# Three signals for a unit's transposed components, and a quad's compression in one run, in the sample-score stage of a hybrid decoder step

## The reference

```python
def compress_blocks(kseq, pe, w1, w2):          # CMP_STRIDE 16, HD 64
    ...
    ch = kp.reshape(B, nc, CMP_STRIDE, KH, HD).transpose(0, 1, 3, 2, 4).reshape(B, nc, KH, CMP_STRIDE * HD)
    ha = ch @ w1[:half]
    hb = ch @ w1[half:]
    h = ha[:, :-1] + hb[:, 1:] + pe.reshape(-1) @ w1
    return jax.nn.silu(h) @ w2
```

## Time and profile before

| | us |
|---|---|
| timed runs, median of 3 | 3030.18 (3027.63 to 3040.13) |
| profiled execution | 3035.08 |
| its span | 3033.3 |
| TensorE busy | 2729.7 (90%) |
| its weight loads busy | 2222.7 (73%) |
| DVE / ACT / POOL busy | 917.5 / 577.9 / 238.8 |
| turns, L979, both layers | 216.2 in 1600 records |
| compression, L1009, both layers | 288.8 in 4352 records |

### The profile page before, as it was taken

One profiled execution on the slowest core, in us unless ns is written; L12 is line 12 of the kernel. 1 busy time (PEld: TensorE's weight loads), 2 busy tenths in 40 slices (PEclk: granted clock), 3 DMA queues, 4 the chain that ended last, 5 costly groups with the idle time before them and its releaser, 6 DMA issues. The chain is left out here.

```text
span 3033.3 us, 44988 instructions
## 1 busy us (share of the span) xinstructions
PE 2729.7 (90%) x17236; PEld 2222.7 (73%) x17236; DVE 917.5 (30%) x2207; ACT 577.9 (19%) x1224; POOL 238.8 (8%) x328
## 2 busy tenths in 40 slices
PE   6996999698698999999969879987977989999997
PEld 4875888466585888888758678865757768888885
DVE  2731333443543210000118223343544332010002
ACT  0012332223310200000110223322242103000002
POOL 0500000000030100000005000000002101000000
PEclk8997999799695999999979979997987879999998
DMA  6205775242001134022042256733410021341220
GB/s 194 75 28 151 212 216 176 73 123 81 2 22 50 44 109 125 28 69 71 0 138 70 49 177 215 217 112 105 125 48 1 22 91 35 108 122 28 56 56 30
DMA packets 343596, 276.93 MB, mean 91 GB/s; under 512 B 61473, under 2 KB 339106, under 8 KB 343002
## 3 DMA queue, kind: packets, MB, share of 16 engines
q1 hardware_dynamic: 316840, 253.71, 28.4%
q10 hardware_dynamic: 26546, 20.35, 2.2%
HBM read 264.14 MB, written 18.17 MB: 93 GB/s over the span
## 5 line engine op out<-in xcount | busy, mean ns | idle before, releaser
L2166 PE MATMUL psum<-xT,up_ring 128*128 128x272 f32 x2048 | 470.3, 392 | 0.0
L2166 PEld LDWEIGHTS psum<-xT,up_ring 128*128 128x128 f32 x2048 | 389.0, 190 | 80.3
L2185 PE MATMUL psum<-ff,HT 128*128 128x272 f32 x1536 | 353.6, 392 | 0.0
L2185 PEld LDWEIGHTS psum<-ff,HT 128*128 128x128 f32 x1536 | 291.8, 190 | 60.2
L368 PE MATMUL psum<-xT,w_ring 128*128 128x272 f32 x1408 | 327.4, 396 | 7.4 <-PEq L161 4.0
L368 PEld LDWEIGHTS psum<-xT,w_ring 128*128 128x128 f32 x1408 | 269.7, 192 | 65.0 <-issue 4.7
L979 PE MATMUL psum<-cst,cache 128*128 128x128 f32 x1600 | 216.2, 286 | 14.0 <-DMA cache<-in_cache_nsa_kv 10.8
L979 PEld LDWEIGHTS psum<-cst,cache 128*128 128x128 f32 x1600 | 181.1, 146 | 32.9 <-DMA cache<-in_cache_nsa_kv 11.2
L2029 DVE SCALAR_TENSOR_TENSOR xT<-xT,psum 128x544 f32<-128x544 f32 (+1 forms) x42 | 24.2, 584 | 529.5 <-PE psum L2185 441.6
L1009 PEld LDWEIGHTS psum<-chunks,W 64*128 64x128 f32 x2304 | 144.0, 199 | 24.0 <-issue 24.0
L1009 PE MATMUL psum<-chunks,W 64*128 64x128 f32 (+1 forms) x2304 | 157.3, 289 | 0.0
(11 more groups left out here) (423 smaller groups left out, 3161.0 us busy)
## 6 DMA issues: line engine op xcount, KB each, us to landing
cache<-in_cache_nsa_kv SPq DMA_DIRECT2D x512, 192.0 KB, 2.7
up_ring<-in_w_up SPq DMA_DIRECT2D x32, 1024.0 KB, 5.1
vsel<-in_cache_nsa_kv SPq DMA_DIRECT2D x384, 64.0 KB, 1.9
HT<-in_w_down SPq DMA_DIRECT2D x12, 2048.0 KB, 9.0
w_ring<-in_w_in SPq DMA_DIRECT2D x20, 1024.0 KB, 5.0
vsel<-in_cache_nsa_kv ACTq DMA_DIRECT2D x128, 64.0 KB, 2.2
HT<-in_w_out SPq DMA_DIRECT2D x8, 1024.0 KB, 6.6
yT<-in_w_down SPq DMA_DIRECT2D x4, 2048.0 KB, 10.3
```

The costliest lines, as they stand in the source:

```text
L2166: last = pe.matmul(psum[:, 2 * (t % 4) + h, 0:HALF], up_ring[:, g % 3, k, (t % 2) * P:(t % 2) * P + P], xT[:, k, half_of(h)], start=(k == ...
L2185: last = pe.matmul(psum[:, 2 * (t % 4) + h, 0:HALF], down[t % 3][:, k, :], f[:, k, half_of(h)], start=(k == 0), stop=(k == FT - 1))
```

## The change

The signal `turned` becomes three: `sel_turned`, `k_turned` and `v_turned`, each set at the fourth transpose of its component. ACT and DVE wait for the component that they copy. SyncE reloads a slot at `v_turned`, the last one (`sel_turned` for window units). On TensorE the four parts of a quad's compression are no longer spread over the four turns: all four stand in one run of 128 records behind the second unit of the next quad and behind `score`.

```diff
-    names = ("turned", "k_copied", "v_copied", "sel_act", "sel_dve", "scored", "sc_copied", "tok", "pe_turned", "pe_copied",
+    names = ("sel_turned", "k_turned", "v_turned", "k_copied", "v_copied", "sel_act", "sel_dve", "scored", "sc_copied", "tok", "pe_turned", "pe_copied",
...
                 if u >= slots:
-                    sp.wait_ge(s.turned, u - slots + 1)
+                    sp.wait_ge(s.v_turned if paged(u - slots) else s.sel_turned, u - slots + 1)
...
                     for j in range(gp):
                         last = pe.transpose(psum[:, bank, j * P:j * P + P], cache[:, u % slots, j, c * P:c * P + P], C["ident"])
-                last.then_inc(s.turned, 1)
+                    last.then_inc((s.k_turned, s.v_turned, s.sel_turned)[c], 1)
...
                     turn(4 * q + i)
                     if i == 1 and q:
                         score(q - 1)
-                    if q <= NQD:
-                        compress(q - 1, i)
+                    if i == 1 and q <= NQD:
+                        for part in range(4):
+                            compress(q - 1, part)
...
             for u in range(NU):
                 q, i = u // 4, u % 4
-                act.wait_ge(s.turned, u + 1)
                 if u % 2 == 0:
+                    act.wait_ge(s.sel_turned, u + 1)
...
                 if paged(u):
+                    act.wait_ge(s.k_turned, u + 1)
...
-                dve.wait_ge(s.turned, u + 1)
                 if u % 2:
+                    dve.wait_ge(s.sel_turned, u + 1)
...
                 if paged(u):
+                    dve.wait_ge(s.v_turned, u + 1)
```

## The result

| | before | changed |
|---|---|---|
| median of the timed runs, us | 3035.3 (3027.6 to 3040.1) | 3103.7 (3095.0 to 3110.9) |
| span of the profiled execution, us | 3033.3 | 3095.6 |
| TensorE's first turn to the key products (L1025), layer 1 / layer 2 | 261.3 / 261.5 | 293.9 / 292.4 |

The changed kernel takes 1.0225 times the time of before (95% interval 1.0202 to 1.0248): 68 us more where 55 were forecast. The spans of the two profiled executions differ by 62 us, and the two runs through the stage by 32.6 and 30.9 us, so in the profiles nothing of it lies elsewhere.

A forecast was written before the change was run, and what follows sets the result against it. TensorE's own order of work was taken to bound the kernel. 2 x (25.0 - 7.7 + 4.1) = +43 us, plus 12 for clock falls, made +55: 3085 us on the timed runs' scale, range 3050 to 3122.

The forecast's parts named there:

- The bound and the cause: Stage `scores`: TensorE's own order of work sets the pace; in the old order loads are early and copies hidden.
- D's load: Load of the fourth of four units turned in a row (4q+5); can't be issued before the first is turned.
- The load, 5.3 us: From the first unit's end to the fourth's data landed: 0.61, 1.7 and 3.0 us, 5.3 in all; bounds 4.6 and 5.8.
- D's wait: TensorE stands about 2.5 us once a quad before the fourth unit in a row, with nothing to cover it.
- The run: Compression's 128 records in one run: 7.35 us in place of 7.94 a quad, at 0.056 us a record.
- The rival of tighter runs: Unbroken compression runs (L1009) pack tighter: at 0.042 us a record 3012 us, faster than before; 4 in 100.
- The step: New quad, from one first unit's end to the next's: 16.56 us, +1.79; over 14 steps +25.0 us a layer.
- The clock after a wait: In `scores`, 7 of 30 new waits drop the clock, 1.7 us lost each: +12 us, bounds none and +38.
- The rival in which most waits bring it down: Clock falls at 24 of 30 new waits, 2.5 us lost each: +103, 3133 us; 15 in 100.
- The first quad: First matmul to first scores: 28.4 becomes 20.7 us with an early clock rise, a gain of 7.7 a layer.
- The last quads: Units 64 to 71, one bank and one DMA each: two steps of 14.0 and 13.3 us for 23.2, +4.1 a layer.
- The signals: Three separate signals: worth nothing in the old order; in the new, 0 to 0.3 us a unit lies under the wait.

The follow-up runs named there:

- e7_split_issue: Changed kernel, but two of the four DMAs of every fourth unit in a row are issued by ACT beside SyncE's two; 3106.9 us.
- e9_split_and_hold: Changed kernel with two of the fourth unit's four DMAs issued by ACT and the next load held back one turned unit; 3098.1 us, single execution.
- e10_hold: Changed kernel with only the load behind the fourth unit's held back until the third unit has been turned; 3105.7 us, single execution.
- after: Profile of the changed kernel itself, three signals and one run of 128 records, against the kernel before; median 3103.7 us, ratio 1.0225.
- e2_run_only: Kernel before with only the order changed: the run of 128 records with the old single signal; 3120.4 us, ratio 1.0279.
- e8_two_runs_one_signal: Kernel before with two runs of 64 records a quad and the old single signal; 3093.6 us, ratio 1.0208.
- e4_two_runs: Changed kernel with two runs of 64 records, behind a quad's second and fourth units, three slots and three signals; 3017.2 us, ratio 0.9937.

## Why the prediction was right, point by point

- **The bound and the cause.** Loads early and copies hidden before; D's load late after. Shown by the fourth slot, in one program.
- **The load, 5.3 us.** Measured 5.43 on average from A's end to D's start (4.74 to 6.71, 30 of them). The total was right, and so were the times of its parts, but not the reading of them as a sum: with the issue made 1.0 us shorter the total stayed, so a forecast for two queues by the same sum missed by that much. The Trainium skill's "DMA: Bandwidth & Descriptors", section "Anatomy of one DMA — SWDGE (gpsimd) path", with a fixed cost of about 2.0 us, put the landing at 2.4 us. That section fits DMAs issued by GpSimd, and these are issued by SyncE, which the prediction did not say; from the fourth issue to D's start it was 3.0 us, and 4.0 with the issue split over two queues.
- **D's wait.** Expected 2.5 us a quad, measured 2.0 (1.1 to 3.7, 60 us in all). The load took as long as expected, but more of it was covered: at every second quad C itself waits 0.63 us for DVE's copy, where the prediction had 0 to 0.3 us a unit. Under D's wait this costs nothing, as said; with the fourth slot it shows.
- **The run.** 7.35 us expected, 7.34 to 7.35 measured at full clock. The steady pitch of rows 3 and 4 holds over 128 records. The rival of tighter runs is out.
- **The step.** 16.56 us without falls of the clock, and 12 us of falls over 28 steps, make 16.99; measured 17.05.
- **The clock after a wait.** Seven falls expected in the steady part, seven found (near 309, 378 and 412 us, and four in the second layer). That the count is exact is luck: the quarter was a choice between none and most, and three runs with the same waits or shorter ones have two (`e7_split_issue`), six (`e9_split_and_hold`) and five (`e10_hold`). One of them, in the trace of the changed kernel:

```profile
309.30:312.70 3.40, 2.97 (x16) 2.62 (x20) 0.80 (x2) 0.59 (x1) 0.16 (x1) 0.50 0.89 261
```

  It begins within the wait and ends some 3 us later in dense work, so about 1.5 us is lost, near the 1.7 counted. The rival in which most waits bring it down is out in all these traces; what decides which wait does is open.
- **The first quad.** Expected a gain of 7.7 us a layer, measured 4.8 and 5.8 (first scores after 23.6 and 22.7 us). This term was mis-sized: the run of 34 wide was taken at the full clock throughout. In the trace of the changed kernel it has both levels, 2.4 GHz from 275.2 and 1.2 GHz from 282.0 to 288.8 us:

```profile
275.20:282.00 6.80, 6.80 (x115) 6.63 (x113) 1.38 (x2) 0.59 (x1) 0.00 (x0) 1.00 0.86 261
282.00:288.80 6.80, 6.80 (x48) 6.73 (x46) 1.19 (x2) 1.17 (x2) 0.00 (x0) 0.50 0.01 3
```

  The premise was off as well: turns 0 and 1 are not without a break, since the second unit's load leaves 0.54 us between them in the first layer; the clock rose all the same. The time of the rise differs from run to run by itself: 21.4 us after the first turn in the profile of before, 15.4 us in that of the signals alone, with the same order and first scores at 28.4 and 25.5 us. With the changed order the first scores of four profiles (`after`, `e7_split_issue`, `e9_split_and_hold`, `e10_hold`) come after 22.2 to 26.2 us, 24.2 on average, so the gain over an average run of before is smaller still, about 3 us a layer.
- **The last quads.** Expected +4.1 us, measured +3.8 (13.34 + 13.68 against 23.18). Not in the sum: the step behind them, where the clock fell among the short turns, 10.3 and 7.8 us against 6.9; up to the key products it costs 1.6 and 0.8 us.
- **The signals.** Worth nothing in the old order, as said. In the new one they lie under D's wait, as said, but for some 0.3 us in D's start; their worth in another order had not been asked.

In all, 55 us were forecast and the profiles show 63.5 in the stage: 5 of the difference are the first quads, 2 the end, 2 the steps. The 68 us of the medians are 5 more, within what single profiles differ from medians. The forecast of 3085 us besides stood on a median of before of 3030.2 us, which was 3035.3 with more executions; so some 5 of the 19 us between 3085 and 3103.7 lie there.

## What to carry to other kernels

When work is gathered into one long run, count what is now gathered between two runs: with n slots, n units in a row are the most that the loads can feed, and the next load's whole time stands open. The time of one load is read from the end of the unit that frees the slot to the first matmul on the new data, not from the share of DMA over the stage. Split the run so that each stretch of slots has cover longer than one load (here 6.6 us against 5.4 on average, and even then one load a layer came late): two runs took the gain of merging (0.4 us a quad) without the wait, and only then were separate signals worth having.

## What the runs showed of the hardware

- A load of 768 KB by itself filled the 16 DMA engines for 2 us (98%, 340 GB/s, read in one load of `e9_split_and_hold`), and its time from freed slot to first matmul was 5.4 us on average whether one queue issued the four DMAs in 1.7 us or two queues in 0.6.
- A run of 128 records with a moving side of 34 let the clock fall from 2.4 to 1.2 GHz 3 to 6 us after its start, though the records show TensorE busy throughout.
- At the start of the stage, turns with a gap of 0.77 us between them left the clock at 1.2 GHz for 35 to 36 us in three of four layers (`e2_run_only`, `e8_two_runs_one_signal`) and for 3.6 us in the fourth.
- Of 30 waits of TensorE of 1.1 to 3.7 us in dense work seven came with a fall of the clock to 1.2 GHz for 3.4 us each (changed kernel).
- In a pair of turns with one signal the copy costs 0.77 us of idle (ACT); with a signal for each bank it costs none (`e4_two_runs`). Where four turns stand in a row, 0.63 us stay at every second quad (DVE).
